# A transformer and RWKV7/mixture block: seven products for V, the recurrence's output norm reordered, experts and combine in one block

## The reference, cut to what matters

```python
# first block (DEPTH 1): forgetting attention, then a gated MLP
h = rms_norm(x, norm_mix) * (1 + sc_m) + sh_m
proj = h @ w_in                        # q, k, v (3 x 1024 columns) and 16 gate columns
q, k = rms_norm(q, q_g), rms_norm(k, k_g)      # per head of 64
F = cumsum(log_sigmoid(f_pre + b_f))
o = softmax(q.k * scale + F[t] - F[s], s <= t) @ v
x = x + g_m * (o @ w_out)
x = x + g_f * (square(relu(h2 @ w_mlp_in)) @ w_mlp_out)
# second block: pool and rwkv7, then a mixture of 32 experts
#   state = state*decay + (state @ -kk) (kk*a)^T + v k^T ; y = state @ r, 12 heads of 64
y = (y - mu) * rsqrt(var + LNX_EPS) * lnx_g + lnx_b       # output norm, per head
y = (y + bonus) * g
h = layer_norm(ALPHA * x + mixed, ln1)
ffn = sum over 2 of 32 experts: weight * (silu(h @ gate) * (h @ up)) @ down
out = layer_norm(ALPHA * h + ffn, ln2)
```

## Time and profile before

| what | value |
|---|---|
| median of 3 runs | 3013.24 us (3011.2 to 3014.5) |
| the profiled execution | 3023.13 us, its span 3021.4 us |
| mean granted clock of TensorE | 0.975 |
| PE busy, whole span | 2836.5 us (94%) |
| attention, 381 to 667 us | PE 260.49 of 286 |
| MLP, 667 to 1650 us | PE 973.27 of 983 |
| recurrence, 1650 to 2384 us | PE 687.67 of 734, DVE 482.44, ACT 313.13 |
| experts, 2558 to 2951 us | PE 377.31 of 393, DMA share 0.88 |
| combine and the pause ahead of it, 2951 to 3021 us | PE 44.20 of 70, DVE 38.83 |

### The profile page before, as it was taken

How to read it: one execution, slowest core, us unless ns; L and a number is a source line. 1 busy time by engine, 2 the same in 40 slices (tenths; PEclk the granted TensorE clock), 3 DMA queues, 4 the chain that set the end, 5 groups by cost and what they waited for, 6 DMA issues and landing times. The chain is left out here.

```text
span 3021.4 us, 48468 instructions
## 1 busy us (share of the span) xinstructions
PE 2836.5 (94%) x18832; PEld 1851.9 (61%) x18832; DVE 1538.4 (51%) x4129; ACT 725.1 (24%) x1635; POOL 265.6 (9%) x343
## 2 busy tenths in 40 slices
PE   4999989999999999999999999999999896999996
PEld 3886456664588544886444777777777554444442
DVE  5543056771355566655564666666666466111115
ACT  3211055551210000000002344444444200111111
POOL 0000011100000000000000122222222100010002
PEclk7999999999999999999999999999999897999998
DMA  5010033321022453224443100000000121999965
GB/s 224 29 47 38 0 105 99 108 83 42 14 84 84 167 181 139 84 86 162 161 177 144 57 25 26 2 26 16 12 25 2 50 87 43 351 358 352 355 242 195
DMA packets 103937, 338.62 MB, mean 112 GB/s; under 512 B 6944, under 2 KB 16672, under 8 KB 94640
## 3 DMA queue, kind: packets, MB, share of 16 engines
q1 hardware_dynamic: 96816, 310.55, 28.6%
q0 software_dynamic: 6912, 25.17, 2.3%
HBM read 302.60 MB, written 33.10 MB: 111 GB/s over the span
## 5 line engine op out<-in xcount | busy, mean ns | idle before, releaser
L1854 PE MATMUL mixing_ps<-all_main,pre_ws 128*128 128x256 f32 x1152 | 315.5, 397 | 0.0
L1189 PE MATMUL mlp_ps<-mlp_w2s,all_main 128*128 128x512 f32 x512 | 239.6, 592 | 0.0
L2790 PE MATMUL ex_pg<-all_main,ex_xT 128*128 128x512 f32 x512 | 226.9, 596 | 0.0
L1854 PEld LDWEIGHTS mixing_ps<-all_main,pre_ws 128*128 128x128 f32 x1152 | 200.0, 189 | 30.3
L1189 PE MATMUL mlp_ps<-all_main 128*128 128x512 f32 x384 | 183.2, 593 | 0.7 <-DVE all_main L1402 0.7
L2790 PEld LDWEIGHTS ex_pg<-all_main,ex_xT 128*128 128x128 f32 x512 | 98.0, 192 | 123.3 <-issue 123.3
L1189 PEld LDWEIGHTS mlp_ps<-mlp_w2s,all_main 128*128 128x128 f32 x512 | 96.6, 190 | 117.8 <-issue 104.6
L2180 POOL TENSOR_TENSOR all_tail<-all_tail,pre_cst 128x256 f32<-128x256 f32 x120 | 103.6, 878 | 430.5 <-DVE all_tail L2236 290.0
L1189 PEld LDWEIGHTS mlp_ps<-all_main 128*128 128x128 f32 x384 | 72.6, 190 | 93.4 <-issue 68.5
L2924 DVE TENSOR_TENSOR ex_hid<-ex_pg,ex_sil 128x256 f32<-128x256 f32 x32 | 13.6, 425 | 223.8 <-ACT ex_sil L2872 223.8
L1139 PE MATMUL mlp_ps<-all_main,all_early 128*128 128x256 f32 x512 | 121.0, 379 | 0.0
(11 more groups left out here) (440 smaller groups left out, 5039.8 us busy)
## 6 DMA issues: line engine op xcount, KB each, us to landing
mlp_w2s<-in_w SPq DMA_DIRECT2D x64, 1024.0 KB, 4.9
all_main<-in_w_gu SPq DMA_DIRECT2D x32, 2048.0 KB, 9.3
all_early<-in_w SPq DMA_DIRECT2D x32, 1024.0 KB, 4.9
att_wa<-in_w_ada SPq DMA_DIRECT2D x32, 512.0 KB, 3.7
all_early<-in_w_d SPq DMA_DIRECT2D x16, 1024.0 KB, 10.9
all_main<-in_w_d SPq DMA_DIRECT2D x16, 1024.0 KB, 11.2
y_rows<-ex_y SPq DMA_DIRECT2D x32, 512.0 KB, 3.0
qkv_wq<-in_w_qkv SPq DMA_DIRECT2D x6, 2048.0 KB, 7.7
```

The costliest lines, as they stand in the source:

```text
L1189: last = nc.tensor.matmul(ps[:, PRODUCTS.index(name), :], lhsT=lhsT, rhs=rhs, start=j == 0, stop=j == FPAIRS - 1)
L1854: last = nc.tensor.matmul(ps[:, bank, 0:UT], lhsT=ws[:, n, k, :], rhs=xT[:, k, (col + NB) % S:(col + NB) % S + UT], start=(k == 0), stop=( ...
L2790: last = nc.tensor.matmul(pg[:, n % 2, :], lhsT=xT[:, n % 2, k, :], rhs=gu[n][:, k, :], start=(k == 0), stop=(k == KT - 1))
```

## The change

Three parts, named by what they do.

1. *Projection.* SP loads `wf` and `fb` at the end of the start's list of loads. All six chunks go by seven products. The sums of squares are made for the first four only; the mean squares are made before chunk 4 and the root and inverse after its first pair. The sums `S` and `T` lie in `xres`, so x is overwritten, and attention's SP list loads it again in turn p = 3.
2. *Recurrence.* ACT: root after `x_out(2)` and scalings after `x_out(3)`. DVE: inverse and bias behind `n2`, between `t_in(2)` and `t_in(3)`. PE: the turning back of YN in `between(5)`, ahead of the product with `up`, and `project(2, 2..3)` remains alone in `between(4)`.
3. *Experts and combine* are one block. The norm rows are loaded at its head. DVE makes the diagonals and multiplies `xres` by ALPHA before its first expert step. After the overflow loop each engine goes on with the combine. PE forms only the weighted rows; DVE adds the scaled residual and takes the row sum in one instruction, subtracts the mean and multiplies by the gain in another; ACT squares with a sum for the variance and takes the root; DVE ends with inverse and one instruction that scales and adds the bias.

The diff, cut to its core:

```diff
                     sp.dma_start(main[:, k, 0:2 * D], w_ada[k * P:(k + 1) * P, 0:2 * D]).then_inc(w_in[k], 16)
+                sp.dma_start(wf[:], w_f).then_inc(wf_in, 16)
+                sp.dma_start(fb[:], b_f.rearrange("(h a) -> h a", a=1)).then_inc(wf_in, 16)
...
-    SEVENTHS = 4
+    NORMED = 4
...
-        S1, S2, S4 = ([main[:, 2 * n + k // 2, 2 * D + (k % 2) * NB:2 * D + (k % 2 + 1) * NB] for k in range(HK)] for n in range(3))
+        S1, S2, S4 = ([sums[:, 2 * n + k // 2, (k % 2) * NB:(k % 2 + 1) * NB] for k in range(HK)] for n in range(3))
         T1, T2, T4 = (t.rearrange("p (k c) -> p k c", k=HK) for t in
-                      (main[:, 6, 2 * D:3 * D], main[:, 7, 2 * D:3 * D], gates[:, 0, :]))
+                      (sums[:, 6, :], sums[:, 7, :], gates[:, 0, :]))
...
-                sp.dma_start(wf[:], w_f).then_inc(wf_in, 16)
-                sp.dma_start(fb[:], b_f.rearrange("(h a) -> h a", a=1)).then_inc(wf_in, 16)
                 for n in range(2):
...
                 last.then_inc(mm_f, 1)
-                for c in range(SEVENTHS):
+                for c in range(CHUNKS):
                     pe.wait_ge(w_in[c % 2], 16 * (c // 2 + 1))
...
                             product(c, i, name)
-                pe.wait_ge(part, part_at(SEVENTHS - 1, 2, "c12"))
-                for c in range(SEVENTHS, CHUNKS):
...
                         first(c, i)
-                        for name in SQUARES:
-                            squares(c, i, name)
+                        if c < NORMED:
+                            for name in SQUARES:
+                                squares(c, i, name)
...
+                        if c == NORMED and i == 0:
+                            act.wait_ge(prep, 1)
+                            nc.scalar.activation(norm, norm, ACT.Sqrt).then_inc(root, 1)
...
                     yield
+                def mean_squares():
+                    dve.wait_ge(summed, 16 * NORMED)
...
+                    dve.wait_ge(root, 1)
+                    nc.vector.reciprocal(norm, norm).then_inc(set_up, 1)
...
                         gather(c, i)
                         next(gates_step, None)
-                    if c + 1 < SEVENTHS:
+                        if c == NORMED and i == 0:
+                            inverse_norms()
+                    if c + 1 < CHUNKS:
                         for n in range(4):
                             column_sum(c + 1, n)
-                for k in range(HK):
-                    last = tt(A21[k], A11[k], A21[k], ALU.subtract)
-                last.then_inc(restored, 1)
...
+                    if c + 1 == NORMED:
+                        mean_squares()
+                dve.wait_ge(part, 28 * CHUNKS)
...
                         sp.dma_start(wa[:, c % 2, :], w_ada[k * P:(k + 1) * P, (2 + c) * D:(3 + c) * D]).then_inc(wa_in[c % 2], 16)
+                    if p == 3:
+                        for half in range(2):
+                            sp.dma_start(xres[:, half * TT // 2:(half + 1) * TT // 2, :],
+                                         x[half * NB:(half + 1) * NB, :].rearrange("(t p) d -> p t d", p=P)).then_inc(x_back, 16)
                     sp.wait_ge(maxed, 24 * (p - 1))
...
                         if l == 4:
+                            project(2, range(2, 4), B_BANK)
+                        if l == 5:
                             if prev:
...
-                            project(2, range(2, 4), B_BANK)
-                        if l == 5:
                             if nxt:
...
                         make(fac_exp[:], fac_log[:], ACT.Exp)
+                    x_out(2)
                     if prev:
                         wait(act, dve_y, y, "y_eps")
                         nc.scalar.activation(rstd[:, 1, :], rstd[:, 0, :], ACT.Sqrt).then_inc(act_y.sem, 1)
-                    x_out(2)
+                    x_out(3)
                     if prev:
                         wait(act, dve_y, y, "y_nb")
                         for n in range(4):
                             nc.scalar.activation(YN[:, n // 2, n % 2, :], Y[:, n // 2, n % 2, :], ACT.Identity,
                                                  scale=rstd[:, 1, n:n + 1], bias=rstd[:, 2, n:n + 1]).then_inc(act_y.sem, 1)
-                    x_out(3)
                     if nxt:
...
-                    get(act_y, y, "y_root", prev)
-                    norm(None, rec, rstd[:, 1, :], rstd[:, 1, :])
-                    norm("y_inv", stt, out=rstd[:, 2, :], in0=mv[:, :, 0], scalar=-1.0, in1=rstd[:, 1, :], op0=ALU.mult, op1=ALU.mult)
                     t_in(2)
                     get(pe_a, u, "kk_sum", nxt)
                     get(act_w, q, "b3", win and nxt)
                     make(None, ts, n2[:].rearrange("p w h -> p (w h)"), ps[:, 5, 0:4], 2.0, 2e-24, ALU.mult, ALU.max)
                     make("sq_max", rec, n2[:].rearrange("p w h -> p (w h)"), n2[:].rearrange("p w h -> p (w h)"))
+                    get(act_y, y, "y_root", prev)
+                    norm(None, rec, rstd[:, 1, :], rstd[:, 1, :])
+                    norm("y_inv", stt, out=rstd[:, 2, :], in0=mv[:, :, 0], scalar=-1.0, in1=rstd[:, 1, :], op0=ALU.mult, op1=ALU.mult)
...
+                for n in range(2):
+                    sp.dma_start(rows[:, n, :], ln_rows[n].partition_broadcast(P)).then_inc(r_in, 16)
                 for n in range(2):
...
+                for t in range(TT):
+                    sp.wait_ge(ready, t + 1)
+                    sp.dma_start(out_rows[t * P:(t + 1) * P, :], hres[:, t, :]).then_inc(stored, 16)
+                sp.wait_ge(stored, 16 * TT)
...
+                for n in range(2):
+                    pool.wait_ge(y_out[n], 16 * (EXPERTS // 2 + 1))
+                pool.sem_inc(gate, 1)
+                for t in range(TT):
+                    if t >= RING:
+                        pool.wait_ge(summed, t - RING + 1)
+                    for c in range(2):
+                        nc.gpsimd.indirect_dma_start(out=yg[:, t % RING, c, :], out_offset=None, in_=y_dram,
+                                                     in_offset=bass.IndirectOffsetOnAxis(ap=dest[:, c, t:t + 1], axis=0)
+                                                     ).then_inc(g_in[t % RING], 16)
...
+                def weigh_rows(t):
+                    pe.wait_ge(g_in[t % RING], 32 * (t // RING + 1))
+                    if t >= RING:
+                        pe.wait_ge(added, t - RING + 1)
+                    for half in range(2):
+                        for c in range(2):
+                            last = nc.tensor.matmul(ps[:, 2 * (t % RING) + half, :], lhsT=diag[:, c, t, :],
+                                                    rhs=yg[:, t % RING, c, half * NB:(half + 1) * NB], start=(c == 0), stop=(c == 1))
+                    last.then_inc(summed, 1)
...
+                pe.wait_ge(weighed, 2 * TT)
+                for t in range(TT):
+                    weigh_rows(t)
...
+                for t in range(TT):
+                    act.wait_ge(centre, t + 1)
+                    if t >= 2:
+                        act.wait_ge(squared, t - 1)
+                    nc.scalar.activation(xT[:, t % 2, :, :].rearrange("p a b -> p (a b)"), hres[:, t, :], ACT.Square, bias=mv[:, t, 1:2],
+                                         accum_out=mv[:, t, 2:3]).then_inc(squared, 1)
+                    act.wait_ge(squared, t + 1)
+                    nc.scalar.activation(mv[:, t, 3:4], mv[:, t, 2:3], ACT.Sqrt, bias=eps[:], scale=1.0 / D).then_inc(rooted, 1)
...
+                def finish(t):
+                    dve.wait_ge(rooted, t + 1)
+                    nc.vector.reciprocal(mv[:, t, 3:4], mv[:, t, 3:4]).then_inc(inverse, 1)
+                    dve.wait_ge(inverse, t + 1)
+                    dve.wait_ge(shifted, t + 1)
+                    nc.vector.scalar_tensor_tensor(out=hres[:, t, :], in0=y[:, t % 2, :], scalar=mv[:, t, 3:4], in1=rows[:, 1, :],
+                                                   op0=ALU.mult, op1=ALU.add).then_inc(ready, 1)
...
+                for t in range(TT):
+                    for c in range(2):
+                        nc.vector.tensor_scalar(diag[:, c, t, :], ident[:], wgt[:, c, t:t + 1], None, ALU.mult).then_inc(weighed, 1)
+                nc.vector.memset(eps[:], LN_EPS).then_inc(scaled, 1)
+                for t in range(TT):
+                    nc.vector.tensor_scalar(hres[:, t, :], hres[:, t, :], ALPHA, None, ALU.mult).then_inc(scaled, 1)
                 dve.sem_inc(pipe.hidden, 2)
...
                 dve.wait_ge(r_in, 32)
+                dve.wait_ge(scaled, TT + 1)
                 for t in range(TT):
                     dve.wait_ge(summed, t + 1)
-                    for c in range(2):
-                        done(nc.vector.bn_stats(stats[:, t, c, :], ps[:, 2 * (t % RING) + c, :]))
-                    done(nc.vector.bn_aggr(mv[:, t, 0:2], stats[:, t, :, :].rearrange("p a b -> p (a b)")))
```

(15 more changed lines are left out.)

189 lines of the change are left out of this document (45 added, 144 removed).

## The result

| | before | after | ratio (95% interval) |
|---|---|---|---|
| median, us | 3013.87 (3011.2 to 3015.65, 4 runs) | 2972.74 (2972.33 to 2975.74, 4 runs) | 0.9866 (0.9849 to 0.9884) |
| profiled execution, us (span) | 3023.13 (3021.4) | 2972.33 (2970.6) | |

The change saves 41.1 us by the medians; 40.3 had been forecast, and 2972.9 for the time. The two profiled executions differ by 50.8 us, more than the kernels do, since the one of before lay 9 us above its median. Most of that excess lies in a stretch with the old code in it: from attention's first turn to the recurrence's first projection product it took 1279.9 us, against 1269.3 to 1272.8 in the five other executions with that code.

A forecast was written before the change was run, and what follows sets the result against it. PE was taken as nearly always busy in every long stage; 1.9 + 12.1 + 13.0 + 15.3 - 2.0 = 40.3 us saved, from the median 3013.24 to 2972.9 us. Range 2963 to 2985, forecast's chance 0.70.

The forecast's parts named there:

- Gate weights: Projection's start: PE starts with DVE instead of behind the bias DMA, 1.9 us saved, between nothing and 5.
- V by seven products: Projection: two seven-product chunks of 48.97 us replace V's 16 plain products of 110.06 us, 12.1 us saved.
- Recurrence: Recurrence: PE's 0.54 us wait for ACT at the second level goes in 24 steps, 13.0 us saved, lower end 6.
- nothing takes its place: Recurrence: no new PE wait follows the removed one, all covers being positive, the smallest 0.3 us.
- Rival (b): Recurrence: the stall moves on and the step stays as long as it is, 2985.9 us; chance 0.08.
- End: Combine after the experts: earlier gathers and tiles of 4.2 us on DVE save 15.3 us, between 12 and 19.
- PE's loop is unchanged and ends near 2963.2: Overflow loop after the experts: PE, not the gathered data (near 2961), is next late; first sum at 2969.4.
- Start of the experts: Experts' start: DVE's diagonals and scalings and SP's norm rows delay the first gathers, a slip of 2.0 us, between 0 and 7.
- rival (a): Experts' start: DVE holds the gathers until 2567.3, slip 7.5 us instead of 2, 2978.4 us; chance 0.12.
- (c): Recurrence: DVE's late bias holds ACT's scalings and PE waits in each step, slower, 3025.7 us at 2.2 us exposed; chance 0.02.
- (d): Merged experts and combine: gathers or PE start no earlier, 8 of the 15.3 us are lost, 2980.9 us; chance 0.08.
- three signs of being wrong: A new PE wait over 5 us, a DVE combine tile over 4.7 us, or gathers later than PE's loop.

The follow-up runs named there:

- the root alone: The kernel before with the changed recurrence's root, copies, inverse and scalings, but the turn-back left at the fourth level: 3015.92 us, ratio 1.0008.
- the three variants with the short pause: The changed kernel with DVE's prologue moved into the pause (2969.67 us), norm rows later (2969.55), or PE alone going round the overflow loop (2969.74).

## Why the prediction was right

**The sum.** By stretches: start 5.2, V 12.2, recurrence 13.8, end 12.9, less a slip of 0.5: 43.6 us, with 40.3 forecast and 41.1 in the medians (35 to 46 by the ratio's interval). The three parts alone give 13.6 + 15.3 + 10.7 = 39.6 by their medians. That they add was a premise, and it held as far as such intervals tell. That the total was met to 1 us is in part luck: the start gave 3.3 us more than its term and the slip took 1.5 less, the end gave 2.4 less, and the medians lie 2.5 below the sum of the stretches.

**Gate weights.** The wait was sized right for the execution shown (1.9), and is 2.4 over several. The term was too small by the clock, 2.3 us, which stood in the text as a possible extra and was left out of the sum: 1.9 forecast, 5.2 measured, just above the bound of 5.

**V by seven products.** 12.1 forecast, 12.2 measured. The chunk measured in the trace of before was the right price for one more of it.

**x reloaded.** 0 forecast, and 35.80 us a turn with and without it; for attention as a whole 1 us can't be told from none.

**Recurrence.** 13.0 forecast, 13.8 in the trace of the changed kernel and 13.7 alone. The step "nothing takes its place" stood on covers of 0.3 us and more, and the order in the trace is the one worked out; the smallest cover, 0.3 us, came out at 0.6 (r's copy ends at 2021.62 and DVE reads it at 2022.18). The size was less sound than it looks. The 24 waits of the earlier trace rows were read as one a step, but 21 of them stand in the steps, 11.8 us together, and three behind the last projection product, where they stay. Against that a step got shorter by more than its 0.54: from one second-level product to that of the next step it was 2047.30 - 2017.42 = 29.88 us and is 2046.92 - 2017.65 = 29.27, 0.61 less. The two errors nearly cancel. What the prediction did not say is how much hung on the turn-back: it named it as over 2 us of cover, and with the turn-back left at the fourth level the cover is -0.7 us and the whole 13 us are lost. Rival (b), the stall that moves on, is exactly what the root alone does.

**End.** 15.3 forecast, 12.9 measured. The step that failed is "PE's loop is unchanged and ends near 2963.2", 12.4 us after the last copy: it took 15.5. With cold products of 6.2 the first sum was forecast 18.6 us after the last copy; the three variants with the short pause have 18.5, 18.6 and 18.8, the changed kernel itself 21.6. So the mechanism (PE late, not the data) was right, and the 3.1 us above it are the open ones. The step took for granted that PE's unchanged code needs its unchanged time, and the runs show that it need not. A tile was forecast at 4.2 and is 4.05; from the first sum to the end of DVE it is 33.1 us for a forecast of 33.6, which gives 0.5 back.

**Start of the experts.** 2.0 forecast. The wait grew by 1.1; from DVE's last step before the stage to the last expert's copy it is 392.0 to 393.0 us in six executions with the old start (392.3 in the mean) and 392.6 to 392.9 in four with the new one (392.8), so 0.5 remains; with the norm rows later it is 392.1, and with DVE's part moved away 393.5, no shorter. The prediction had weighed two causes. It was the norm rows: without them PE waits 6.35 us, without DVE's part 7.47.

**DVE beside POOL's gathers.** DVE's scalings do touch POOL: its third gather took 1.22 us to issue beside them and its small index copies 0.51 and 0.53 us, where without DVE the gather took 0.96 and the copy 0.19. With the prologue moved into the pause it is the combine's gathers that take longer, 1.34 us for the first and 1.01 for the next three, against 0.94. The rule of the Trainium skill (SBUF — State Buffer, the trap that DVE blocks DMA) points at the right engines, and its effect here is some tenths of a microsecond an instruction; rival (a), 7.5 us, did not come, and the wait was as long with DVE's work as without it (7.44 and 7.47 us). That POOL gets its turn between DVE's 0.7 us instructions would explain it; no run tests that.

**Rivals (c) and (d).** No wait for the scalings shows in the recurrence. The gathers did start earlier; of (d) only PE's part came true, 3.1 of the 8 us.

**The signs.** None of the three signs of being wrong came. Three of the signs of being right came out otherwise: the combine's first matmul was to come within 13 us of the last copy and came after 15.5; a step of the recurrence was to fall from 29.4 to 28.9 us and fell from 29.9 to 29.3; and PE's first product of the experts was to lie 8 to 12 us behind DVE's last step, where the first turning lies 7.2 us behind it and the first up-product 12.1.

## What to carry to other kernels

When a wait is taken out of a loop, ask of each thing that is moved by it how late the next waiter would then stand, and move that one too: here each half alone brought nothing and both 15 us. A loop that goes round with nothing to do can be work on the path like any other; look in the pauses of all engines for it, and put one condition around it (6 us here, of which PE's own rounds are at least 2.3 and 3.1 are unexplained). Work for an idle engine belongs where the next thing queued behind it is far, not merely where the engine is idle.

## What the hardware showed that was not expected

- A pause of PE of 3.3 to 4.6 us cost 1.7 to 2.9 us more in the products behind it, at a granted clock of 0.50 in place of 1.00; one of 1.4 us cost nothing. In the last expert a pause of 3.9 us cost 2.7 more on eight products.
- Identical PE code with a loop of 15 empty rounds took 15.5 us in two executions and 12.3 to 12.4 in three, where only other engines' code differed. The cause is open.
- Two loads of 512 KB, issued 1.1 us ahead of a gather, made the gather come 1.1 us later.
